# Order of the first loads: constants and identity behind the page and weight transfers, and ScalarE's page loads ahead of the first square root

## The reference, cut to what matters

```
h = rms_norm(x, norm1_g)                       # first norm
z = h @ w_in                                   # 1024 x 1864
u, q, k, v, iq, ik, iw = split(z)
q = rope(rms_norm(q, q_norm_g)); k = rope(rms_norm(k, k_norm_g))
iq = rope(iq); ik = rope(ik); iw = iw * 8**-0.5
# sample tokens: score = sum_h relu(iq_h . idx_key) * iw_h over 1024 paged + 4 new keys
# top 256 keys per query, attention over them; pooling mixer; output projection; residual
x = x + peer(rms_norm(x, norm2_g))             # product-key retrieval over 16384 experts
```

## Time and profile before

| | |
|---|---|
| time, median of 3 runs | 1020.89 us (1019.98 to 1027.91) |
| the profiled execution | 1021.0 us, of it the span of the trace 1019.3 us |
| TensorE matmul busy | 993.5 us (97%) |
| VectorE busy | 752.7 us (74%) |
| ScalarE busy | 513.9 us (50%) |
| Pool busy | 437.0 us (43%) |

### The profile page before, as it was taken

How to read it: one execution, slowest core, us unless ns; L and a number is a source line. 1 busy time by engine, 2 the same in 40 slices (tenths; PEclk the granted TensorE clock), 3 DMA queues, 4 the chain that set the end, 5 groups by cost and what they waited for, 6 DMA issues and landing times.

```text
span 1019.3 us, 18359 instructions
## 1 busy us (share of the span) xinstructions
PE 993.5 (97%) x6050; PEld 837.9 (82%) x6050; DVE 752.7 (74%) x1542; ACT 513.9 (50%) x1070; POOL 437.0 (43%) x330
## 2 busy tenths in 40 slices
PE   5999999999999999999999999999999999999998
PEld 1447778889999999999999998878888788888886
DVE  2559999739998926666777775778788778888773
ACT  2123322343455567777777775655454445545442
POOL 4653344235688876666666663012122211112210
PEclk9999999999999999999999999999999999999999
DMA  9535568458755554444444446588888878888872
GB/s 330 126 110 182 163 193 317 152 187 309 265 181 184 166 186 144 142 138 140 143 141 143 144 144 218 208 329 306 276 296 298 293 261 308 301 299 308 293 261 89
DMA packets 75021, 221.11 MB, mean 217 GB/s; under 512 B 11301, under 2 KB 23213, under 8 KB 74564
## 3 DMA queue, kind: packets, MB, share of 16 engines
q1 hardware_dynamic: 60636, 179.25, 51.6%
q0 software_dynamic: 13040, 40.52, 12.0%
q10 hardware_dynamic: 1280, 0.53, 0.3%
HBM read 217.31 MB, written 3.14 MB: 216 GB/s over the span
## 4 chain that ended last, share of the span: by engine, by line
PE 76%; DVE 12%; issue 3%; POOL 3%; DMA 3%; SPq 2%; ACT 1%; ACTq 0%; POOLq 0%; DVEq 0%
PE psum L1056 32%; PE psum L988 15%; PE psum L993 10%; PE psum L992 6%; PE psum L1004 6%; DVE top L1608 4%; DVE work_s L1609 4%; POOL w_lo L1501 3%; PE psum L573 3%; DMA w_rest<-w_in_blocks 2%; PE psum L818 2%; DMA w_raw<-expert_v 1%; SPq L419 1%; DVE work_p L1609 1%; DMA raw_more<-expert_v 1%
## 5 line engine op out<-in xcount | busy, mean ns | idle before, releaser
L1501 POOL TENSOR_TENSOR w_lo<-w_raw,w_hi 128x1024 fp32r<-128x1024 f32 x116 | 277.4, 2396 | 136.5 <-ACT w_hi L1099 136.5
L1099 ACT ACTIVATE w_hi<-w_raw 128x1024 fp32r<-128x1024 f32 x214 | 228.4, 1068 | 160.4 <-PE psum L1056 96.3
L993 PE MATMUL psum<-h_split,w_lo 128*128 128x256 f32 x1024 | 287.6, 281 | 0.0
L988 PE MATMUL psum<-h_split,w_hi 128*128 128x512 f32 x640 | 232.1, 403 | 0.0
L993 PEld LDWEIGHTS psum<-h_split,w_lo 128*128 128x128 f32 x1024 | 194.5, 190 | 0.0
L1056 PE MATMUL psum<-w_hi,ag_hi 128*128 128x512 f32 x512 | 158.3, 390 | 2.1 <-DVE ag_lo L1883 2.1
L1056 PE MATMUL psum<-w_hi,ag_lo 128*128 128x512 f32 x512 | 157.8, 389 | 0.0
L1876 DVE TENSOR_TENSOR w_lo<-w_raw,w_hi 128x1024 fp32r<-128x1024 f32 x98 | 120.5, 1229 | 39.8 <-ACT w_hi L1099 39.6
L992 PE MATMUL psum<-h_split,w_hi 128*128 128x256 f32 x768 | 140.2, 285 | 1.4 <-issue 1.2
L988 PEld LDWEIGHTS psum<-h_split,w_hi 128*128 128x128 f32 x640 | 120.3, 188 | 25.6
L992 PEld LDWEIGHTS psum<-h_split,w_hi 128*128 128x128 f32 x768 | 119.4, 192 | 2.9 <-issue 2.8
(11 more groups left out here) (294 smaller groups left out, 1464.1 us busy)
## 6 DMA issues: line engine op xcount, KB each, us to landing
w_raw<-expert_ut SPq DMA_DIRECT2D x128, 512.0 KB, 3.5
w_raw<-expert_v SPq DMA_DIRECT2D x86, 512.0 KB, 4.5
raw_more<-expert_v SPq DMA_DIRECT2D x42, 512.0 KB, 4.8
w_slice<-w_pq_cols SPq DMA_DIRECT2D x32, 512.0 KB, 6.2
w_most<-w_in_blocks SPq DMA_DIRECT2D x8, 699.0 KB, 12.6
w_slice<-w_o_half SPq DMA_DIRECT2D x8, 512.0 KB, 4.2
v_cache<-cache_v POOLq DMA_DIRECT2D x64, 64.0 KB, 3.2
w_o_sb<-w_o_half SPq DMA_DIRECT2D x8, 512.0 KB, 7.7
```

What stands on the lines that cost most here:

```text
L988: pe.matmul(psum[:, 2 + s, :], w_hi[:, s, c, :], h_split[:, c].rearrange("p a t -> p (a t)"), start=(c == 0), stop=False, skip_group_check ...
L993: mm = pe.matmul(out, w_lo[:, s, c, :], h_split[:, c, 0], start=False, stop=(c == KC - 1), skip_group_check=wide)
L1099: return act.activation(out, in_, ACT.Copy)
L1501: pool.tensor_tensor(w_lo[:, s], w_raw[:, s], w_hi[:, s].bitcast(F32), ALU.subtract).then_inc(S["w_lo_ready"], 1)
```

## The change

Four moves, with no instruction added or removed except that VectorE's wait for the constants moves with them:

- SP issues `ident` behind the 16 transfers of `w_in` and not ahead of them.
- ScalarE issues its 16 pages behind its squares and ahead of the wait for the first root.
- Pool issues its 24 pages ahead of the seven constants.
- VectorE waits for the constants only at L1591, in `rope_qk`, ahead of the product with `gain5`; the copy to `iota16` and the fold to `fold4` move behind the rotary of the first prompt tile, ahead of the wait for the sample scores.

```diff
--- before.py
+++ after.py
@@ -414,10 +414,10 @@
 
             for k in range(0, KC, 2):
                 sp.dma_start(xT[:, k:k + 2, :], x_t[:, k:k + 2, :]).then_inc(S[f"x_in{k // 2}"], 16)
-            sp.dma_start(ident[:], c_ident).then_inc(S["ident_in"], 16)
             for k in range(KC):
                 sp.dma_start(w_most[:, k], w_in_blocks[k, :, 0:3, :]).then_inc(S[f"w_in_in{k}"], 16)
                 sp.dma_start(w_rest[:, k], w_in_blocks[k, :, 3, :]).then_inc(S[f"w_in_in{k}"], 16)
+            sp.dma_start(ident[:], c_ident).then_inc(S["ident_in"], 16)
             sp.wait_ge(S["gains_in"], 16 * len(gain_loads))
             ik_loads(sp, 0, W_IK[0])
             sp.dma_start(keysT[:], keys_t).then_inc(S["keys_in"], 16)
@@ -1102,11 +1102,10 @@
             for c in range(KC):
                 act.wait_ge(S[f"x_in{c // 2}"], 16)
                 act.activation(sq[:, c, :], xT[:, c, :], ACT.Square).then_inc(S["sq_ready"], 1)
+            act.wait_ge(S["gains_in"], 16 * len(gain_loads))
+            ik_loads(act, W_IK[0] + W_IK[1], W_IK[2])
             act.wait_ge(S["rstd_half"], 1)
             act.activation(rstd_a[:, 0:12], rstd_b[:, 0:12], ACT.Sqrt).then_inc(S["rstd_root"], 1)
-
-            act.wait_ge(S["gains_in"], 16 * len(gain_loads))
-            ik_loads(act, W_IK[0] + W_IK[1], W_IK[2])
 
             def head_root(i, n):
                 act.wait_ge(S["head_var"], i + 1)
@@ -1435,10 +1434,10 @@
             pool.memset(ones[:, :], 1.0).then_inc(S["ones_set"], 1)
             for dst, src in gain_loads:
                 pool.dma_start(dst, src).then_inc(S["gains_in"], 16)
+            pool.wait_ge(S["gains_in"], 16 * len(gain_loads))
+            ik_loads(pool, W_IK[0], W_IK[1], "ik_in_pool")
             for dst, src in early_loads:
                 pool.dma_start(dst, src).then_inc(S["consts_in"], 16)
-            pool.wait_ge(S["gains_in"], 16 * len(gain_loads))
-            ik_loads(pool, W_IK[0], W_IK[1], "ik_in_pool")
             pool.wait_ge(S["consts_in"], 16 * len(early_loads))
 
             for i, t in enumerate(ORDER):
@@ -1567,15 +1566,9 @@
             dve.tensor_tensor(sq[:, 0, :], sq[:, 0, :], sq[:, 4, :], ALU.add).then_inc(S["sq_summed"], 1)
             dve.wait_ge(S["ssq_done"], 1)
             inverse_mean(rstd_b[:, 0:12], psum[:, 4, 0:12], D, S["rstd_half"])
-            dve.wait_ge(S["consts_in"], 16 * len(early_loads))
-            dve.tensor_copy(iota16[:, :], iota[:, :]).then_inc(S["iota16_ready"], 1)
-            dve.wait_ge(S["ident_in"], 16)
-            dve.tensor_reduce(fold4[:, :], ident[:].rearrange("p (j t) -> p t j", t=NS), AX, ALU.add
-                              ).then_inc(S["fold4_ready"], 1)
 
             def rope_qk(i):
 
-                dve.wait_ge(S["consts_in"], 16 * len(early_loads))
                 t = ORDER[i]
                 n = TILES[t][1]
                 if t < 2:
@@ -1588,6 +1581,7 @@
                 inverse_mean(small[0:n, 8:8 + NH + 1], small[0:n, 0:NH + 1], HD, S["head_var"])
                 dve.wait_ge(S["head_root"], i + 1)
                 settle(dve.tensor_tensor(x, x, bc(small[0:n, 16:16 + NH + 1], 2, HD), ALU.mult))
+                dve.wait_ge(S["consts_in"], 16 * len(early_loads))
                 settle(dve.tensor_tensor(x, x, gain5[0:n], ALU.mult))
                 x = z[0:n, t, O_Q:O_V].rearrange("p (h a d) -> p h a d", a=2, d=HD // 2)
                 cos, sin = (bc(rope[0:n, t, o:o + HD // 2], 1, NH + 1) for o in (0, HD // 2))
@@ -1661,6 +1655,10 @@
 
 
             dve.tensor_copy(fold16[:], fold[:])
+            dve.tensor_copy(iota16[:, :], iota[:, :]).then_inc(S["iota16_ready"], 1)
+            dve.wait_ge(S["ident_in"], 16)
+            dve.tensor_reduce(fold4[:, :], ident[:].rearrange("p (j t) -> p t j", t=NS), AX, ALU.add
+                              ).then_inc(S["fold4_ready"], 1)
             dve.wait_ge(S["score_s_copied"], 1)
             settle(dve.tensor_tensor(score_s[:, PAST:KEYS], score_s[:, PAST:KEYS], causal_new[:, :], ALU.add))
             def norm2_p(_):
```

## The result

The changed kernel takes 1029.68 us (median of 22 runs, 1026.62 to 1033.81), the kernel before 1024.96 us in the runs beside it. The ratio is 1.005, interval 1.0031 to 1.0068: 5.1 us slower (3.2 to 7.0), where the forecast was 3.4. Within 1%, as forecast, but the median lies above the range of 1021.6 to 1028.0. Part of that is the base: the three runs that the forecast started from have a median of 1020.89, the 22 (these three and 19 more) one of 1024.96. The profiled execution is 1028.81 us, its span 1027.1 against 1019.3.

What follows compares the result with a forecast made beforehand. The opening's chain through TensorE to the sample scores was taken to bound, any delay there coming out whole. 1021.0 + 3.4 for late constants = 1024.4 us, sooner weights and VectorE's gain not counted; range 1021.6 to 1028.0.

Steps and rivals of the forecast that it cites:

- the mechanism: Opening: late constants delay Pool's and VectorE's rotaries, TensorE waits for Pool; sample scores and the end come 3.4 us later.
- the landing of `gain5`: Last constant on Pool's queue: issued at 42.5, landing 3.3 us later, with bounds of 2.0 and 7.1.
- the rival of held-up issues: VectorE's instructions hold up each of Pool's seven constant issues: 5.6 us more, 1030.0; chance 4%.
- Constants in at 45.8: Opening, behind Pool's pages: all constants landed at 45.8 us (44.5 to 49.6), from where both rotaries shift.
- so I leave 9.98 where it is: Pool's first page group hangs on the gains, not the seven issues, so still starts at 9.98; sixth ends at 39.10.
- "hidden" rival: Gains 2 us sooner and a 2.0 us landing put the constants in by 42.5: not slower, 1020.7; chance 9%.
- Pool's rotary 6.2 us: Pool's indexer rotary begins at 45.9 instead of 39.20 and is done at 52.1, 6.7 us later.
- TensorE at full speed behind the wait: TensorE waits until 52.1, ends its sample transposes by 53.1, then begins the half unit 3.4 us later than before.
- ScalarE's pages at 0.35 us: Weights: four more of ScalarE's 32 KB pages ahead of the last block take back 0.35 us.
- the same number serves for that: Base: profiled execution of 1021.0 is 0.1 above the runs' median, so 1024.4 serves as forecast for the median too.
- the bounds of 2.1 to 7.2: Delay of the half unit ahead of the sample scores, 3.4 us, bounded by the last constant's landing time alone.
- the slow restart: Rival: TensorE restarts slowly after its 4.9 us wait ahead of the transposes, adding 2.1 us: 1026.5; chance 25%.

Runs made afterwards that it cites:

- Pool's move alone: Changed kernel with only Pool's and VectorE's moves kept, identity and ScalarE's pages as in the kernel before; ratio 1.0044.
- the kernel with the eight spare matmuls: Kernel before plus eight matmuls whose result nobody reads, on TensorE ahead of the sample transposes; ratio 1.0067.
- that with six spare matmuls: Changed kernel plus six matmuls whose result nobody reads, ahead of TensorE's wait for Pool's indexer rotary; ratio 1.0056.
- the one with slow scores: Changed kernel with the first half of prompt unit 4 moved ahead of TensorE's wait instead of behind the transposes; ratio 1.0056.

## Why the prediction was right or wrong

**Right: the mechanism.** The constants behind Pool's pages, the wait of both engines for them, of TensorE for Pool, and the delay handed on to the last stage: all there, and Pool's move alone gives it. Right too the landing of `gain5` (3.3 forecast, 3.1 measured), the unchanged pace of the page groups, ScalarE's pages (11.1 to 31.7 forecast, 11.15 to 30.3 measured), and its root (33.2 forecast, 32.0 measured). The seven issues took 3.3 us from first to last, as before, but this says little on the rival of held-up issues: VectorE stood idle from 39.4 to 47.4, so none of its instructions ran beside them (in Pool's move alone one did, at 40.34 for 0.81 us, and they took 3.3 us too). What speaks against that rival is Pool's page groups, which kept their 2.42 us with VectorE at work from 33 to 39.

**Wrong: the size.** Scores at 56.4 were forecast, 60.96 came, 4.6 us more. By terms, in the profiled execution:

- *Constants in at 45.8; it was 47.4, 1.6 us more.* The step was "so I leave 9.98 where it is". The gains landed at 8.0 and Pool's first group began at 11.62. Across the profiles here the gains landed between 6.3 and 8.0 us, in the changed kernel at 8.0, 6.6 and 6.9, so most of this term looks like chance of the one execution. That they would land sooner without the constants behind them, which fed my "hidden" rival, showed nowhere.
- *Pool's rotary 6.2 us; it took 6.9 from 47.41 to 54.33, and 6.9 to 7.0 in the six other profiles with Pool's constants late.* I moved the row of before as it stood, and 6.2 was itself the least of the five profiles with early constants (6.2 to 6.7); with the constants on ScalarE it was 7.3. In the row of before Pool started ahead of VectorE's rotary, and now one landing lets both go together: the second to fourth product, 0.8 us each before, took 1.0 to 1.35, while the two behind them went from 1.26 and 1.36 to 0.92 and 1.03. The third tile's rotary in the kernel before, with VectorE idle beside it, has 0.79 or 0.80 for each of the same six (timeline of Pool, before):

```profile
59.12 0.79 POOL L1456 TENSOR_TENSOR idx_tmp<-z,rope 128x288 f32<-128x288 f32 x1 [5.65 <-ACT z L1121]
...
62.99 0.79 POOL L1461 TENSOR_TENSOR z<-idx_tmp 128x288 f32<-128x288 f32 x1
```

That the overlap with VectorE causes it is argued from these timelines, and no run isolates it.
- *TensorE at full speed behind the wait.* The sum had "does nine transposes, then five, by 52.9", and the half unit at its old 3.3 us. The transposes took 1.6 instead of 1.0 and the half unit 4.9: 2.2 us. This is the step that failed in kind: I had the price (2.1, from the first block) and gave it 25%. It came in each of the four profiles with such an idle time, and even after 3.8 us of it. The Trainium skill, "TensorE: Matmul & The Clock Gate", Part 1, tells of a fall to 1.2 GHz after idle; the granted clock of 0.56 agrees. I let the doubt of the trace, which had no such idle time to show, stand against a case whose only precedent, the start of this kernel, was slow.

1.6 + 0.8 + 2.2 = 4.6 in the opening. With gains at 6.4 (Pool's move alone) the scores came at 60.0, 7.0 us late. The three ratios, 1.0044, 1.0050 and 1.0058, say 4.5 to 5.9 us; 7.0 is at the upper end of the second interval, inside the third and above the first. Part of the difference is the profiled execution of before, whose opening was an early one: the kernel with the eight spare matmuls, the same up to there, was 0.8 us later. The rest stays open.

**Wrong without effect: ScalarE's pages at 0.35 us.** By themselves, with the constants early, they went with 1.1 us at the scores; in the changed kernel the wait covered whatever they cost. The size is rough, since the landing of the weights alone moved the opening by 0.8 us between two profiles with the same opening. Where constants and pages are not both ahead of the last blocks, as in the version with the constants on ScalarE, TensorE waits for weights 10.9 us instead of 13.8 and a gain of 1.4 to 2.0 us is left. That the two loads together are what costs is argued from these waits; no run isolates it.

**The range.** What put the measured 1029.68 outside 1021.6 to 1028.0 was the base: the step "the same number serves for that". From 1024.96 even the forecast's own 3.4 gives 1028.4, and from 1020.89 the measured ratio gives 1026.0, inside. Three runs between 1019.98 and 1027.91 had announced a base as loose as that. So the change in time, 5.1 us against 3.4 and within the bounds of 2.1 to 7.2, was forecast better than the opening, 7.9 against 3.4; that the time shows less of the miss than the trace has no cause that the runs show, so it counts as luck. The range had the slow restart inside at 1026.5, but not together with a late landing.

## What to carry to other kernels

Issues that stand ahead of a wait for something slower cost nothing, as Pool's seven did while it waited for the gains (its first page group began 3.6 us behind their landing with the seven ahead of it and 3.6 without); the same seven behind the wait were 3.3 us plus a landing on the path. Move them to a queue with idle time before their first use, not to the end of the queue that is last to finish. And where a change makes TensorE stand for as long as here (3.8 to 7 us), count the slow spell behind it as part of the wait, not as a rival.

## What the runs showed of the hardware

**The clock.** After 7.0 us without work the granted clock of the stretch from 53 to 60 us was 0.56 and TensorE needed 1.5 times as long for its half unit; after 3.8 us it was 0.50, the 1.2 GHz level, in the same stretch, and the scores took 1.9 times as long (3.64 against 1.92 us). With spare matmuls up to 0.5 us before the transposes, it was 1.00.

**Where the time varies.** The last stage is the value half of the experts. Here are the starts of the first and the last of its matmuls that read `ag_lo`, in the kernel before, the changed kernel, that with six spare matmuls and that with Pool's order undone:

```profile
L1056 PE MATMUL psum<-w_hi,ag_lo x512: 389/389/398, 657.8 to 1013.4; 128*128 128x512 f32 x171
```
```profile
L1056 PE MATMUL psum<-w_hi,ag_lo x512: 387/389/398, 665.5 to 1021.2; 128*128 128x512 f32 x171
```
```profile
L1058 PE MATMUL psum<-w_hi,ag_lo x512: 387/389/398, 663.3 to 1022.5; 128*128 128x512 f32 x171
```
```profile
L1056 PE MATMUL psum<-w_hi,ag_lo x512: 387/389/398, 658.8 to 1019.3; 128*128 128x512 f32 x171
```

These are 355.6, 355.7, 359.2 and 360.5 us for the same instructions; over all fourteen profiles 354.6 to 361.3. The stage from the scores to the last top-256 round was 136.0 or 136.1 us in all but the one with slow scores (139.1), and the stage of the `i_hot` by `j_hot` matmuls (L1004) 232.8 or 232.9 in all. The first expert chunks took 157.9 to 159.9. So most of the spread between executions, which hides a change of 2 us in the time, sits in the last stage, and a change in the opening is read better from its own place in the trace.
